# Four neighbouring rows of an expert matrix on each partition: first layer's experts and second layer's down matrix

## The chip, the cores and the metric

The kernel runs on one NeuronCore of a Trainium2 chip. The metric is the device time of one execution in microseconds (us), the median of several. Two numbers of the clock of the matrix engine are used below: it is granted 2.4 GHz or half of that, 1.2 GHz, and the profile writes this as 1.00 and 0.50.

The engines are TensorE (PE: matrix products; PEld is its loading of the stationary operand), VectorE (DVE), ScalarE (ACT), GpSimd (POOL) and SyncE (SP), which issues most DMA transfers. SBUF is the memory on the chip, with 128 partitions; PSUM, in 8 banks, takes the products.

## The reference

A chain of two transformer blocks on 256 tokens of 1024 values, all in float32. Only the two mixtures of experts matter here:

```python
# first layer: 16 experts, each token goes to 2 of them
for e in range(N_EXPERTS):
    h = jax.nn.silu(t @ w_gate[e]) * (t @ w_up[e])
    y = y + gate_dense[:, e:e + 1].astype(t.dtype) * (h @ w_down[e])
...
# second layer: 32 experts, each token goes to 4 of them; one block of tokens of one expert
gu = xb @ w_gu[e] + b_gu[e]
gate, up = gu[:, :D_FF_EXPERT_2], gu[:, D_FF_EXPERT_2:]
gate = jnp.minimum(gate, SWIGLU_LIMIT)
up = jnp.clip(up, -SWIGLU_LIMIT, SWIGLU_LIMIT)
glu = gate * jax.nn.sigmoid(SWIGLU_ALPHA * gate)
return ((up + 1.0) * glu) @ w_down[e] + b_down[e]
```

Each expert has three matrices of 1024 x 1024 floats, 4 MB each. Ahead of each mixture stands a token mixer (attention, retention), a normalization and a router that picks the experts.

## The kernel before

**Phases.** The program is written out by hand, engine by engine, with semaphores between the engines; nothing is reordered by a scheduler. Four phases follow each other: a (the first layer's token mixer, and conditioning for the second), m1 (the first layer's experts), b (the second layer's token mixer), m2 (the second layer's experts).

**The ring.** All weights pass through `ring`, six slots of 2 MB (16 KB on each partition), loaded by SP in the order of their use. SP waits for a slot to be free (L979: `sp.wait_ge(S(f"{m}_free{j}"), i + 1)`), issues the transfer of one tile, and goes to the next. In m1 and m2 a slot holds half a matrix, 512 rows of 1024 floats: slots 0 and 1 gate, 2 and 3 up, 4 and 5 down. In the code these halves are cut by `moe_units` (L299 to L306). Its `(k p)` puts row 128k + p of a half on partition p at place k, so each partition receives four separate rows of 4 KB.

**The expert loop.** `moe` (L659) runs once for each block of up to 64 tokens of one expert; a table of blocks, computed on the chip, gives their number and experts. In this run there are 16 blocks in m1 and 32 in m2. The first block's six tiles are loaded ahead of the loop, those of the others within it. On TensorE one pass does this:

- gate products, first half (L694, slot 0). The stationary operand is a chunk of the gathered tokens (128 rows of the model dimension x 64 tokens, from `xgT`), the moving one 512 columns of the weights. Two products with 64 columns each go into the two halves of a PSUM bank.
- `scatter` (L702): adds the previous block's result to the tokens; VectorE sums it up (L1703).
- gate, second half, and up (L694, slots 1 to 3). In m2 a bias comes first (L686).
- `gather` for the next block (L678): x transposed and picked in one go. For each of the 8 chunks `k` of the model dimension and each of the 2 tiles `t` of tokens, 128x128 values of the tokens are the stationary operand and a matrix of zeros and ones, `pick` (128 x 64), the moving one. The source `src` is `x_rows` in m1 and `n2_rows` in m2.
- the turning (L737): the hidden values `hid` (64 tokens in two halves on 128 partitions, 512 columns) are transposed in four chunks with `tp`, and VectorE copies them to `hidT` (L1752). The values to be transposed are the stationary operand, `ident` the moving one. L741 turns the scatter matrix.
- down products (L694, slots 4 and 5), stationary `hidT`.

A matrix product sums over partitions, so chunk k of the stationary operand has to carry the same 128 rows, in the same order, as place k of the weight tile. In m1 the gathered tokens `xgT` are used as they come. In m2 they are first scaled and shifted by vectors that lie chunk by chunk (`sc2` and `mod`, L1688 and L1692).

The profile records each float32 product as two loads and two multiplies, so the 16 products of a gather are 32 records; a transpose is one of each.

Of the kernel before, what the change touches and what calls it, by code (L numbers as in the profile page):

```python
# [2 lines left out]

# [11 lines left out]
P = 128  # L29
# [9 lines left out]
CAP = 64  # L39
# [81 lines left out]
def two_block_kernel(nc, a, consts, bias_rows, out):  # L121

    with ExitStack() as ctx:
# [59 lines left out]
        ident, ones, before, suffix, flip = C("ident"), C("ones"), C("before"), C("suffix"), C("flip")  # L183
# [24 lines left out]
        pick = B(3, 128, 1536).rearrange("p (t s) -> p t s", t=TC)  # L208
        pick_g = B(3, 256, 1664).rearrange("p (t f s) -> p t f s", t=TC, f=2)
        y_slot, hid, up_1, gate_1 = (B(4, 512, 512 * i) for i in range(4))  # L210
# [88 lines left out]
        def moe_units(m, e):  # L299

            if m == "m1":
                cut = [(w, 0) for w in (a["w_gate"][0], a["w_up"][0], a["w_down"][0])]
            else:
                cut = [(a["exp_w_gu_2"][0], 0), (a["exp_w_gu_2"][0], FF), (a["exp_w_down_2"][0], 0)]
            return [w[bass.ds(e, 1), 512 * i:512 * i + 512, lo:lo + 1024].rearrange("o (k p) f -> p (o k) f", p=P)
                    for w, lo in cut for i in range(2)]  # L306

        MOE = {"m1": (E1, NB1), "m2": (E2, NB2)}
        FIRST_SLOT = {"a": 0, "m1": len(units_a), "b": len(units_a), "m2": len(units_a) + len(units_b)}
# [58 lines left out]
        def _(pe):  # L368
            mm = nc.tensor.matmul
            tp = nc.tensor.transpose  # L370
# [85 lines left out]
            for u, kind in enumerate(("q_sb", "k_sb", "v_sb", "q_dl", "k_dl", "v_dl")):  # L456
                w = part("a", u, KC, 512)
# [201 lines left out]
            def moe(m, src):  # L659
# [5 lines left out]
                XG, G, U, DN, Y0, Y1, PT, HT = banks  # L665
# [6 lines left out]
                weights = [part(m, j, 4, 1024) for j in range(SLOTS)]  # L672
                half = [slice(f * CAP, (f + 1) * CAP) for f in range(2)]

                def gather():
                    for k in range(KC):
                        for t in range(TC):
                            i = mm(XG[:, k * CAP:(k + 1) * CAP], src[:, t, k * P:(k + 1) * P], pick[:, t, :],  # L678
                                   start=(t == 0), stop=(t == TC - 1))
                    i.then_inc(S(f"{m}_gathered"), 1)  # L680

# [33 lines left out]
                with pe.Fori(0, n) as i:  # L715
                    if biased:
                        pe.wait_ge(S(f"{m}_expert"), i + 1)
                        biases()
                    pe.wait_ge(S(f"{m}_xgT"), i + 1)
                    pe.wait_ge(full[0], 16 * i + 16)  # L720
                    product(G, token_chunks, 0, biased)

                    pe.wait_ge(S(f"{m}_y_slot"), i + 1)
                    pe.wait_ge(S(f"{m}_put"), i + 1)
                    scatter(4 * i)
                    pe.wait_ge(full[1], 16 * i + 16)
                    product(G, token_chunks, 1, biased)
                    for j in (2, 3):
                        pe.wait_ge(full[j], 16 * i + 16)
                        product(U, token_chunks, j, biased)  # L730

                    pe.wait_ge(S(f"{m}_pick"), i + 2)
                    gather()

                    pe.wait_ge(S(f"{m}_hid"), i + 2)
                    for c in range(4):
                        ins = tp(HT[:, c * P:(c + 1) * P], hid[:, c * P:(c + 1) * P], ident)  # L737
                    ins.then_inc(S(f"{m}_turned"), 1)
                    pe.wait_ge(S(f"{m}_pick_g"), i + 1)
                    for t in range(TC):  # L740
                        ins = tp(PT[:, t * P:(t + 1) * P], pick_g[:, t, :, :], ident)  # L741
                    ins.then_inc(S(f"{m}_put_ps"), 1)
                    pe.wait_ge(S(f"{m}_hidT"), i + 1)
                    for j in (4, 5):
                        pe.wait_ge(full[j], 16 * i + 16)
                        product(DN, hid_chunks, j)
# [31 lines left out]
            for h in range(RH):  # L778
                n = UB["rv", h]
                by_rows([("rv", h, j) for j in range(4)], "b", n, part("b", n, KC, RV), both, RV)  # L780
                for jp in range(2):
                    ps = open_tile(pe, ("S", h, jp))
                    for j in range(2):
                        for c in range(2):
                            at = (2 * jp + j) * P
                            i = mm(ps[:, j * T:(j + 1) * T], rkT[:, 2 * h + c, at:at + P], rqT[:, 2 * h + c, :],  # L786
                                   start=(c == 0), stop=(c == 1))
# [5 lines left out]
                for t in range(TC):  # L793
                    ps = open_tile(pe, ("ro", h, t))
                    for j in range(4):
                        i = mm(ps[:, :], dec2[:, j, t * P:(t + 1) * P], rv[h % 2][:, j, :], start=(j == 0), stop=(j == 3))  # L796
# [16 lines left out]
            for name, cs in ((("cqT", 0), (0, 1)), (("cqT", 1), (2,))):  # L813
                ps = open_tile(pe, name)
                for c in cs:
                    for t in range(TC):
                        i = tp(ps[:, (c % 2) * T + t * P:(c % 2) * T + (t + 1) * P], cqn[:, t, c * P:(c + 1) * P], ident)
                filled(i, name)
            pe.wait_ge(S("ckn_ready"), 4)
            for c in range(2):  # L820
                ps = open_tile(pe, ("ckT", c))
                for j in range(4):
                    i = tp(ps[:, j * P:(j + 1) * P], ckn[:, j, c * P:(c + 1) * P], ident)
# [3 lines left out]
            for j in range(4):  # L827
                i = tp(ps[:, j * P:(j + 1) * P], kr2[:, j, :], ident)
# [8 lines left out]
            for u in range(2):  # L837
                n = UB["uq", u]
                w = part("b", n, 3, 768)
                landed("b", n)  # L840
                for hp in range(2):
                    name = ("qn", 2 * u + hp)
                    ps = open_tile(pe, name)
                    for j in range(2):
                        f = (2 * hp + j) * (NOPE + ROPE)
                        for k in range(3):
                            i = mm(ps[:, j * T:(j + 1) * T], w[:, k, f:f + NOPE], cqnT[:, k, :], start=(k == 0), stop=(k == 2))
                    filled(i, name)
                for t in range(TC):
                    name = ("qr", u, t)  # L850
                    ps = open_tile(pe, name)
                    for k in range(3):
                        heads = w[:, k, :].rearrange("p (h f) -> p h f", h=4)[:, :, NOPE:]
                        i = mm(ps[:, 0:256].rearrange("p (h f) -> p h f", h=4), cqnT[:, k, t * P:(t + 1) * P], heads,
                               start=(k == 0), stop=(k == 2))
# [4 lines left out]
            w = part("b", n, 2, 2048)  # L860
            landed("b", n)
            for h in range(MH):
                ps = open_tile(pe, ("kn", h))
                for k in range(2):
                    f = h * (NOPE + MV)
                    i = mm(ps[:, :], w[:, k, f:f + NOPE], cknT[:, k, :], start=(k == 0), stop=(k == 1))
# [1123 lines left out]
```

## Time and profile before

| | |
|---|---|
| median of 3 runs | 2461.43 us |
| lowest and highest | 2459.41 and 2461.56 us |
| span of the profiled execution | 2460.9 us |
| TensorE busy, multiplies | 2272.0 us (92%) |
| TensorE busy, loads | 1058.3 us (43%) |
| VectorE, ScalarE, GpSimd busy | 591.0, 291.1, 30.8 us |
| moved by DMA | 713.11 MB, mean 290 GB/s |
| TensorE's mean granted clock | 0.964 |

The costliest group is the expert products of L694: 4608 multiplies, busy for 1021.8 us at a mean of 597 ns, with 37.0 us of idle time ahead of them. The gather of L678 has 1600 of each, 195.8 us for the multiplies and 188.9 us for the loads. Multiplies overlap, so the durations of single ones add up to more than the time that passes; the distance between starts is what counts.

A row of the timeline merges neighbouring instructions of a kind: start, length in us, engine, line, operands with buffer numbers left out (`ring` weights, `pool` the work buffers, `bank` PSUM, `cst` constants), and how many; in brackets the idle time ahead of it and who ended it. A load is written `PEld ... LDWEIGHTS`. Time to landing of a DMA runs from its issue to its last byte, so it includes the queue ahead of it.

### The profile page before, as it was taken

What the parts mean: (1) busy time and instruction counts of PE and PEld (TensorE: products, weight loads), DVE (VectorE), ACT (ScalarE), POOL (GpSimd) and SP (SyncE); (2) the same over time, 40 slices, a digit from 0 to 9 for tenths busy, and PEclk for the clock granted to TensorE, in tenths of its full rate; (3) what the DMA queues carried; (4) which work ended last, traced back from release to release, by engine and by line L of the source; (5) the groups of instructions that cost most, each with busy time, mean ns of one, the idle gap of its engine ahead of it and who ended that gap; (6) DMA issues with size and microseconds to landing.
All of it is one profiled execution on the core that took longest, in us unless ns stands there. A gap on an engine that the chain in (4) does not pass through costs nothing.

```text
span 2460.9 us, 24961 instructions
## 1 busy us (share of the span) xinstructions
PE 2272.0 (92%) x9929; PEld 1058.3 (43%) x9929; DVE 591.0 (24%) x1270; ACT 291.1 (12%) x460; POOL 30.8 (1%) x49
## 2 busy tenths in 40 slices
PE   8997699999998999999999599999999999999997
PEld 6654333333335444445545333333333333333333
DVE  0124311122113300001142422222222222222223
ACT  1411000000011021211032000000000000000000
POOL 1000000000000000000000000000000000000000
PEclk9978699999999999999999689999999999999999
DMA  9483399999997311132412169999999999999993
GB/s 347 174 329 153 131 407 410 410 410 410 410 410 278 137 69 69 54 134 103 172 68 84 68 240 397 399 393 399 399 396 397 400 399 398 396 400 396 398 397 153
DMA packets 198661, 713.11 MB, mean 290 GB/s; under 512 B 6027, under 2 KB 8304, under 8 KB 198208
## 3 DMA queue, kind: packets, MB, share of 16 engines
q1 hardware_dynamic: 196704, 707.20, 73.9%
q0 software_dynamic: 1920, 5.40, 0.7%
q8 instruction: 25, 0.41, 0.1%
q14 instruction: 12, 0.10, 0.0%
HBM read 711.52 MB, written 1.06 MB: 290 GB/s over the span
## 4 chain that ended last, share of the span: by engine, by line
PE 48%; issue 45%; DVE 4%; DMA 2%; ACT 1%; SPq 1%; DVEq 0%; POOL 0%; ACTq 0%; POOLq 0%
PE bank L405 14%; PE bank L694 13%; PE bank L423 6%; PE bank L393 3%; PE bank L678 3%; PE bank L702 2%; PE bank L796 1%; PE bank L479 1%; DMA ring<-in_w_up 1%; SPq L979 1%; ACT pool L1082 1%; PE bank L917 1%; DMA ring<-in_ada_w 1%; PE bank L786 1%; PE bank L873 1%
## 5 line engine op out<-in xcount | busy, mean ns | idle before, releaser
L694 PE MATMUL bank<-ring,pool 128*64 128x512 f32 x4608 | 1021.8, 597 | 37.0 <-DVE pool L1752 34.6
L694 PEld LDWEIGHTS bank<-ring,pool 128*64 128x64 f32 x4608 | 320.2, 137 | 699.7 <-issue 648.8
L405 PE MATMUL bank<-ring,pool 128*128 128x512 f32 (+2 forms) x800 | 335.0, 580 | 5.8 <-DVE pool L1780 4.2
L405 PEld LDWEIGHTS bank<-ring,pool 128*128 128x128 f32 x800 | 152.9, 191 | 182.4 <-issue 168.3
L1703 DVE TENSOR_TENSOR pool<-pool,bank 128x512 f32<-128x512 f32 x200 | 128.5, 684 | 352.3 <-PE bank L702 352.3
L678 PEld LDWEIGHTS bank<-pool 128*128 128x128 f32 x1600 | 188.9, 197 | 47.5 <-issue 43.1
L678 PE MATMUL bank<-pool 128*128 128x64 f32 x1600 | 195.8, 282 | 6.9 <-DVE pool L1679 4.3
L702 PE MATMUL bank<-pool,junk 64*128 64x512 f32 x400 | 142.7, 641 | 40.2 <-DVE pool L1703 38.5
L423 PE MATMUL bank<-ring,pool 128*128 128x512 f32 x320 | 141.0, 602 | 10.2 <-ACTq L1084 5.0
L1196 ACT ACTIVATE pool<-bank 128x512 f32<-128x512 f32 x48 | 28.7, 597 | 845.7 <-PE bank L694 845.7
L1082 ACT ACTIVATE pool<-bank 128x512 f32<-128x512 f32 (+1 forms) x121 | 70.4, 582 | 486.4 <-PE bank L405 175.2
L702 PEld LDWEIGHTS bank<-pool,junk 64*128 64x128 f32 x400 | 44.7, 184 | 137.5 <-DVE pool L1703 95.1
L423 PEld LDWEIGHTS bank<-ring,pool 128*128 128x128 f32 x320 | 61.3, 193 | 87.1 <-issue 75.6
L393 PE MATMUL bank<-pool,ring 128*128 128x256 f32 x384 | 85.3, 385 | 3.0 <-issue 2.1
L393 PEld LDWEIGHTS bank<-pool,ring 128*128 128x128 f32 x384 | 73.9, 193 | 15.1 <-issue 3.1
L1193 ACT ACTIVATE pool<-pool 128x512 f32<-128x512 f32 x32 | 20.2, 630 | 374.8 <-DVE pool L1742 374.8
L686 PE MATMUL bank<-pool,junk 32*64 32x512 f32 x256 | 63.6, 615 | 0.0
L1697 DVE COPY junk<-pool 32x64 f32 (+1 forms) x33 | 6.0, 182 | 230.6 <-PE bank L686 230.6
L1746 DVE TENSOR_SCALAR pool<-bank 128x512 f32<-128x512 f32 x32 | 22.1, 692 | 153.2 <-PE bank L694 153.2
L382 PE MATMUL bank<-cst,pool 128*128 128x128 f32 x176 | 27.3, 319 | 26.9 <-DVEq L1539 9.1
L1739 DVE TENSOR_TENSOR pool<-pool,bank 128x512 f32<-128x512 f32 x16 | 11.0, 687 | 158.4 <-PE bank L694 158.4
L1742 DVE TENSOR_SCALAR pool<-bank 128x512 f32<-128x512 f32 x32 | 22.1, 692 | 93.0 <-PE bank L694 93.0
(318 smaller groups left out, 1185.5 us busy)
## 6 DMA issues: line engine op xcount, KB each, us to landing
ring<-in_exp_w_gu SPq DMA_DIRECT2D x128, 2048.0 KB, 10.8
ring<-in_exp_w_down SPq DMA_DIRECT2D x64, 2048.0 KB, 10.3
ring<-in_w_gate SPq DMA_DIRECT2D x32, 2048.0 KB, 17.2
ring<-in_w_up SPq DMA_DIRECT2D x32, 2048.0 KB, 19.4
ring<-in_w_down SPq DMA_DIRECT2D x32, 2048.0 KB, 16.9
ring<-in_w_in SPq DMA_DIRECT2D x22, 2048.0 KB, 14.5
ring<-in_ada_w SPq DMA_DIRECT2D x12, 2048.0 KB, 11.6
ring<-in_w_out SPq DMA_DIRECT2D x4, 2048.0 KB, 15.5
```

Of the source, the lines that this page charges most:

```text
L382: i = tp(ps[:, c * T + t * P:c * T + t * P + P], src[:, t, (2 * cp + c) * P:(2 * cp + c + 1) * P], ident)
L393: i = mm(ps[:, m * T:(m + 1) * T], w[:, k, (2 * mp_ + m) * P:(2 * mp_ + m + 1) * P], src[:, k, :], start=(k == 0), stop=(k == KC - 1))
L405: i = mm(ps[:, 0:width], src[:, k, t * P:(t + 1) * P], w[:, k, 0:width], start=(k == 0), stop=(k == w.shape[1] - 1))
L423: i = mm(ps[t, f][:, :], srcT[:, kk, t * P:(t + 1) * P], w[:, k, f * 512:(f + 1) * 512], start=(kk == 0), stop=(kk == 4 * units - 1))
L479: i = mm(ps[32 * g:32 * (g + 1), :], silc[:, k, :], part("a", n, KC, 512)[:, k, :], start=(k == 0), stop=(k == KC - 1))
L678: i = mm(XG[:, k * CAP:(k + 1) * CAP], src[:, t, k * P:(k + 1) * P], pick[:, t, :], start=(t == 0), stop=(t == TC - 1))
L686: i = mm(dst[half[f], :], this_expert, bgu_rows[:, at:at + 512], start=True, stop=False)
L694: i = mm(dst[half[f], :], chunks[kk], weights[j][:, k, f * 512:(f + 1) * 512], start=(kk == 0 and not biased), stop=(kk == KC - 1))
L702: mm((Y0, Y1)[f][:, :], put[half[f], t * P:(t + 1) * P], y_slot[half[f], :], start=True, stop=True).then_inc(S(f"{m}_scattered"), 1)
L1082: freed(af(dst, view(ps), func, scale=scale), name)
L1196: act.activation(y_slot, DN[:, :], ACT.Copy).then_inc(S(f"{m}_y_slot"), 1)
L1703: tt(ys, ys, (Y0, Y1)[f][:, :], ALU.add).then_inc(S(f"{m}_added"), 1)
```

## The change

Three edits, in two functions. `moe_units` takes the halves of all m1 matrices, and of the down matrix in m2, as `(p k)`: row 4p + k of a half goes to partition p at place k. A partition thus receives four neighbouring rows, which lie in memory as one run of 16 KB. The gate and up matrix of m2 stays `(k p)`; there a row is also half of a longer one (2048 floats), so four of its halves would not be one run. Place k of such a tile holds rows k, 4 + k, 8 + k and so on. So the gather in m1 takes every fourth column of a half of the tokens, from column k on (`tokens_of`), and the turning in both layers every fourth column of `hid`. The number and order of instructions on each engine is the same.

```diff
@@ moe_units
-            return [w[bass.ds(e, 1), 512 * i:512 * i + 512, lo:lo + 1024].rearrange("o (k p) f -> p (o k) f", p=P)
-                    for w, lo in cut for i in range(2)]
+            lay = {True: "o (p k) f -> p (o k) f", False: "o (k p) f -> p (o k) f"}
+            return [w[bass.ds(e, 1), 512 * i:512 * i + 512, lo:lo + 1024].rearrange(lay[m == "m1" or c == 2], p=P)
+                    for c, (w, lo) in enumerate(cut) for i in range(2)]
@@ moe, on TensorE
+                def tokens_of(t, k):
+
+                    if m == "m2":
+                        return src[:, t, k * P:(k + 1) * P]
+                    return src[:, t, 512 * (k // 4):512 * (k // 4 + 1)].rearrange("p (q c) -> p c q", c=4)[:, k % 4, :]
+
                 def gather():
                     for k in range(KC):
                         for t in range(TC):
-                            i = mm(XG[:, k * CAP:(k + 1) * CAP], src[:, t, k * P:(k + 1) * P], pick[:, t, :],
+                            i = mm(XG[:, k * CAP:(k + 1) * CAP], tokens_of(t, k), pick[:, t, :],
                                    start=(t == 0), stop=(t == TC - 1))
                     i.then_inc(S(f"{m}_gathered"), 1)
...
                     for c in range(4):
-                        ins = tp(HT[:, c * P:(c + 1) * P], hid[:, c * P:(c + 1) * P], ident)
+                        ins = tp(HT[:, c * P:(c + 1) * P], hid.rearrange("p (q c) -> p c q", c=4)[:, c, :], ident)
                     ins.then_inc(S(f"{m}_turned"), 1)
```

## Rows read from the trace of the kernel before

**Rows 1.** The page: span, busy time, the 40 slices, packets of DMA.

```profile
span 2460.9 us, 24961 instructions
...
PE 2272.0 (92%) x9929; PEld 1058.3 (43%) x9929; DVE 591.0 (24%) x1270; ACT 291.1 (12%) x460; POOL 30.8 (1%) x49
...
GB/s 347 174 329 153 131 407 410 410 410 410 410 410 278 137 69 69 54 134 103 172 68 84 68 240 397 399 393 399 399 396 397 400 399 398 396 400 396 398 397 153
DMA packets 198661, 713.11 MB, mean 290 GB/s; under 512 B 6027, under 2 KB 8304, under 8 KB 198208
```

**Rows 2.** Timeline of TensorE, one block of the first layer: start, length, engine, line.

```profile
653.52 3.79 PE L678 MATMUL bank<-pool 128*128 128x64 f32 x32
657.14 0.61 PE L737 MATMUL bank<-cst,pool 128*128 128x128 f32 x4
657.58 0.38 PE L741 MATMUL bank<-cst,pool 128*128 128x128 f32 x2
658.69 10.52 PE L694 MATMUL bank<-ring,pool 128*64 128x512 f32 x48 [0.72 <-DVE pool L1752]
...
672.69 10.52 PE L694 MATMUL bank<-ring,pool 128*64 128x512 f32 x48
683.14 3.79 PE L678 MATMUL bank<-pool 128*128 128x64 f32 x32
```

**Rows 3.** The same timeline, the last two blocks of the first layer.

```profile
710.09 3.65 PE L694 MATMUL bank<-ring,pool 128*64 128x512 f32 x16 [0.69 <-DMA ring<-in_w_up]
713.68 3.79 PE L678 MATMUL bank<-pool 128*128 128x64 f32 x32
...
740.80 3.65 PE L694 MATMUL bank<-ring,pool 128*64 128x512 f32 x16 [0.87 <-DMA ring<-in_w_up]
744.39 3.79 PE L678 MATMUL bank<-pool 128*128 128x64 f32 x32
```

**Rows 4.** Waits in the first layer's loop: total us, times, longest.

```profile
PE bank L694 <- DMA ring<-in_w_up: 1.6, 2, 0.9
```

**Rows 5.** Stretches: length, busy of five engines, granted clock, DMA share, GB/s.

```profile
32.00:42.00 10.00, 10.00 (x47) 8.60 (x47) 0.00 (x0) 0.85 (x2) 0.00 (x0) 1.00 1.05 387
409.00:469.00 60.00, 57.02 (x290) 23.89 (x288) 11.43 (x24) 4.95 (x6) 0.00 (x0) 1.00 1.03 410
2000.00:2100.00 100.00, 95.52 (x476) 38.05 (x474) 25.92 (x52) 9.07 (x11) 0.00 (x0) 1.00 1.01 398
```

**Rows 6.** DMA issues by source: count, KB each, median us from issue to landing.

```profile
ring<-in_w_up SPq DMA_DIRECT2D x32, 2048.0 KB, 19.4
...
cst<-shape_constants SPq DMA_DIRECT2D x1, 1392.5 KB, 21.3
...
ring<-in_mla_w_ukv SPq DMA_DIRECT2D x1, 2048.0 KB, 7.6
...
pool<-in_exp_b_gu POOLq DMA_DIRECT2D x1, 256.0 KB, 3.5
```

**Rows 7.** Timeline of TensorE in the second layer: two gathers, one block apart.

```profile
1924.00 3.79 PE L678 MATMUL bank<-pool 128*128 128x64 f32 x32
...
1955.64 3.79 PE L678 MATMUL bank<-pool 128*128 128x64 f32 x32
```

**Rows 8.** Gather and turning: ns minimum/median/maximum, first and last start, form.

```profile
L678 PEld LDWEIGHTS bank<-pool x1600: 186/192/333, 269.9 to 2433.6; 128*128 128x128 f32 x178
L737 PEld LDWEIGHTS bank<-cst,pool x192: 140/142/199, 301.6 to 2434.0; 128*128 128x128 f32 x192
L737 PE MATMUL bank<-cst,pool x192: 272/273/282, 301.7 to 2434.1; 128*128 128x128 f32 x192
```

**Rows 9.** The first gather of the first layer, and the stretches of two gathers.

```profile
269.90 7.09 PE L678 MATMUL bank<-pool 128*128 128x64 f32 x32 [4.27 <-DVE pool L1679]
...
298.05 3.79 PE L678 MATMUL bank<-pool 128*128 128x64 f32 x32
```

**Rows 10.** Stretch around the first of these gathers, columns as in rows 5.

```profile
262.00:277.00 15.00, 10.01 (x46) 9.61 (x46) 3.51 (x12) 0.00 (x0) 0.00 (x0) 0.50 0.00 1
```

## The prediction

> **What bounds the kernel now.** I read the page first, for the whole: TensorE is busy for 92% of a span of 2460.9 us, and the line of GB/s has two plateaus, about 410 from slice 6 to 12 and about 398 from slice 25 to 39 [rows 1]. These are the two expert loops: 16 blocks of the first layer and 32 of the second, six weight tiles of 2048 KB for each block. Two engines could bound such a loop, TensorE or the DMA, so the next view is the timeline of TensorE alone, and in it the distance between equal instructions of neighbouring blocks. Gather to gather, a block of the first layer takes 683.14 - 653.52 = 29.62 us, with no wait for a DMA in it [rows 2]; one of the second layer takes 1955.64 - 1924.00 = 31.64 us [rows 7]. Six tiles are 12.58 MB. In 29.62 us that is a demand of 424.8 GB/s, in 31.64 us one of 397.7.
>
> The view of stretches shows what the DMA gives: 410 GB/s over 60 us of the first layer's loop, and 398 in the second's [rows 5]. In the second loop that is the demand, so TensorE bounds it and the DMA has spare. In the first loop the queue gives less than is asked: a block needs 12.58 / 410 = 30.69 us on the DMA against 29.62 on TensorE. So the transfers fall behind by 1.07 us for each of the 15 blocks that are loaded inside the loop, 16.0 us in all. A tile's median time to landing of 19.4 us there, against 7.6 us for one tile of the middle part, is that queue [rows 6]. The ring of six tiles swallows nearly all of it: only the last two blocks show TensorE waiting for w_up, with gather to gather 30.54 and 30.71 us in place of 29.62, so 0.92 + 1.09 = **2.0 us** [rows 2, 3]; the view of waits agrees in its order (1.6 us) [rows 4]. The slack of the ring was therefore 16.0 - 2.0 = 14 us.
>
> **The change: the transfers.** All 96 tiles of the first layer and the 64 tiles of exp_w_down_2 go from 512 runs of 4 KB to 128 runs of 16 KB. The other 128 tiles of the second layer keep 4 KB. What does a run cost? Units with runs of 2 KB fill the queue at 387 GB/s, runs of 4 KB at 410 [rows 5]. One of the 16 DMA engines thus needs 2048 x 16 / 387 = 84.7 ns for 2 KB and 4096 x 16 / 410 = 159.8 ns for 4 KB. The second 2 KB cost 75.1 ns, so about 9.6 ns of each run do not depend on its size. My estimate for 16 KB is 84.7 + 7 x 75.1 = 610 ns, or **429 GB/s**. A block of the first layer then takes 12.58 / 429 = 29.3 us on the DMA, under TensorE's 29.62: nothing falls behind, and the 2.0 us go. Nothing else can be gained there, because the next limit is TensorE itself, whose own instructions fill the 29.62 us. In the second layer the gain is nothing: no wait for a DMA lies in its loop, and what hides the transfers is the 31.64 us of TensorE against 30.69 of the DMA. The middle part and the start issue the same transfers as before; the middle's first ones come up to 16 us sooner in the queue, but TensorE begins there with the products of the context, for which no wait for a DMA stands in the trace, so I count nothing. On SP the same number of issues stands in the same order.
>
> **The change: the strided reads.** Row 4q + c of a half matrix now lies on partition q in place c, so the other operand has to follow. Nothing is added: the same instructions in the same order, with another address pattern. In the first layer the gather (L678) loads each 128x128 stationary tile from x_rows with a step of four floats, 16 bytes, where it was contiguous. In both layers the turning of hid (L737) does the same. Vector and scalar work, the products and the scatter are untouched. A gather has 32 load and multiply pairs in 657.14 - 653.52 = 3.62 us, 113 ns a pair, while its moving operand has only 64 columns; a load alone lasts 186 to 192 ns [rows 2, 8]. The pair's pace is thus set by the load, and nothing covers it if it becomes longer: TensorE is the bound, and the gather stands on its path in every block. The loads on the path are 17 x 32 = 544 in the gathers of the first layer (one before the loop, one in each block), and 48 x 4 = 192 in the turnings. The turning takes (657.58 - 657.14) / 4 = 110 ns a pair too, but its load lasts only 140 ns against 273 ns of its multiply [rows 2, 8]. There the load has some 46 ns of spare against that of the gather.
>
> No row of this kernel shows a load with a step, so the price is bounded from both sides. Below: nothing, since the stationary tile has the same 128 columns and is delivered to the array at the same pace; a gain is excluded, as fewer bytes or columns are not read. Above: every load at half its pace. The first gather shows what that looks like, 7.09 us against 3.79, with a granted clock of 0.50 around it, that is 1.2 GHz and not 2.4, after an idle stretch [rows 9, 10]. The difference is 3.30 us for 32 pairs, 103 ns a load. On all 544 loads of the gathers that is +56.0 us; on the 192 of the turnings another +19.8 us if they pay alike, and little if their spare hides it. I take **nothing** as the price. The row that argues for it is the turning: its load of the same 128x128 floats lasts 46 ns less than the gather's [rows 8], so the read side of the load can deliver floats faster than the gather asks for them. The gather's pace has then some room before a slower read shows. I give this little more than even weight against the other end.
>
> Here a rule of the Trainium skill speaks against the change. Its page "SBUF — State Buffer", in "Specifications (TRN2)" and again in "Door 1", says that the memory is read in lines of 16 bytes and that an engine needs at least two hits in a line for full bandwidth; a step of four floats has one. The page names no price; if it halves the load's pace here, the sum ends at +74 us instead of -2. No row of the trace bears on it, and the same note also calls four floats a step that is free.
>
> **The sum.** The profiled execution spans 2460.9 us, the median of the three runs is 2461.4, so what holds for the span holds for the median within 0.5 us. Waits -2.0, loads 0, all else 0: 2461.4 - 2.0 = **2459.4 us**.
>
> **The rivals.**
> *The stepped load is slower.* This ends on the other side. Its place is the gather of the first layer and the turning in both; its price is 544x + 192y, x and y being what a load becomes longer. The wait for w_up of 2.0 us vanishes here too, since a block then takes longer than its transfers. At 103 ns for all loads the time is 2461.4 - 2.0 + 56.0 + 19.8 = 2535; if only the gathers pay, 2515. It decides from 10 to 13 ns a load on, where it outgrows 2.0 + 4.9 us. For it: TensorE is the bound and the load sets the pair's pace. Against it: the faster load of the turning. A part of the full price gives 2468 to 2510.
> *The long runs move slower.* Each engine then reads 16 KB from one place before it goes on, and the trace has few such runs. The slack of 14 us covers 15 blocks up to 29.62 + 14 / 15 = 30.55 us; the time is worse than before by over 0.2% once a block needs more than 31.0 us, a rate under 405 GB/s. At 395 GB/s a block takes 31.9 us and the loop waits 15 x 2.2 - 14 = 19 us: 2479. Against it: from 2 KB to 4 KB the rate rises.
> *The runs stay at 4 KB,* if a run of 16 KB is cut on its way. Then the wait stays and the time is 2461.4. Against it: of the 198661 packets 453 are of 8 KB or more [rows 1], and the loads of the constants (128 rows of 11140 bytes), of ukv (256 runs of 8 KB) and of exp_b_gu (32 of 8 KB) make 416 of them if each run is one packet [rows 6]; the other 37 I take for fetches of instructions. A run of 11 KB was not cut.
>
> **How the numbers follow.** Loads free, or under 10 ns each: 0.48, at 2457 to 2462, whether or not runs stay whole. Full price: 0.30, at 2515 to 2535. A part of it: 0.14. Slower runs: 0.03, around 2479. Something gained that I don't see, over 0.2% or 4.9 us: 0.05. A measurement of this kernel can tell about 0.2% from no change. That makes faster 0.05, same 0.48, slower 0.47. The predicted time is that of the likeliest case, whose own range is 2457 to 2462. Since nearly half lies on the slow side and most of that at its far end, the range for 8 in 10 has to reach there: 2457 to 2536.
>
> **What would show it.** The packets should fall by 96 x 384 + 64 x 384 = 61440, to about 137200; if they don't, the third rival holds. In the first layer's loop the GB/s should rise from 410 towards the demand of 425 if the gather keeps its pace, the wait for w_up should be gone and the time to landing of w_up should fall to about half; if the GB/s stay near 410 with waits, the run's size buys nothing. The step that I trust least is read from two numbers: the pair of the gather (113 ns before) and gather to gather (29.62 us before). If these stand at some 216 ns and 33 us, the first rival has won, and the second layer's 31.64 us tell whether the turning pays as well. A load of the turning at 140 ns would say that it doesn't.

## The result, and the profile after

| | before | changed |
|---|---|---|
| median | 2460.54 us (4 runs) | 2550.23 us (4 runs) |
| lowest and highest | 2459.41 and 2461.56 us | 2549.27 and 2554.47 us |
| span of the profiled execution | 2460.9 us | 2552.7 us |
| TensorE's mean granted clock | 0.964 | 0.940 |

The changed kernel takes 1.0367 times as long, 95% interval 1.0352 to 1.0382: **89.7 us slower**, outside the range of 2457 to 2536 us that was given. (The kernel before has one run more here than ahead of the prediction, which puts its median at 2460.54 in place of 2461.43.) The profiled execution is the slowest of the four.

In the changed kernel the same lines have other numbers: the gather is L671 (L678 before), the products L687 (L694), the scatter L695 (L702), the turning L730 (L737). The page first, as in [rows 1]:

```profile
span 2552.7 us, 24961 instructions
...
PE 2370.3 (93%) x9929; PEld 1134.9 (44%) x9929; DVE 592.5 (23%) x1270; ACT 291.2 (11%) x460; POOL 30.8 (1%) x49
...
PEclk9978789888899899999999959999999999999999
...
GB/s 341 181 330 115 144 383 361 355 344 348 365 373 346 135 132 66 67 78 132 103 165 36 121 36 389 396 396 403 396 398 394 402 395 395 399 397 397 398 397 162
DMA packets 137221, 713.11 MB, mean 279 GB/s; under 512 B 6027, under 2 KB 8304, under 8 KB 116288
```

The packets fall by 61440, as counted, and those of 8 KB or more rise from 453 to 20933, by 160 tiles x 128, so the long runs are real. But the plateau of 410 GB/s is gone, and not upwards: 344 to 373 in slices 8 to 12. TensorE asks for less. PEclk falls to 8 in most of the same slices. The timeline of TensorE over one block and the start of the next shows why, to be held against [rows 2]:

```profile
652.93 7.73 PE L671 MATMUL bank<-pool 128*128 128x64 f32 x32
660.45 1.06 PE L730 MATMUL bank<-cst,pool 128*128 128x128 f32 x4
661.31 0.63 PE L734 MATMUL bank<-cst,pool 128*128 128x128 f32 x2
662.29 11.81 PE L687 MATMUL bank<-ring,pool 128*64 128x512 f32 x48 [0.36 <-DVE pool L1745]
...
677.59 10.52 PE L687 MATMUL bank<-ring,pool 128*64 128x512 f32 x48
688.04 7.73 PE L671 MATMUL bank<-pool 128*128 128x64 f32 x32
```

A gather lasts 660.45 - 652.93 = 7.52 us in place of 3.62, 235 ns a pair in place of 113. The second thing stands in the fourth row: 48 products take 11.81 us in place of 10.52, though nothing in them was changed; the 48 after them (677.59) take 10.52 as before. Over the loop the first 48 take from 11.10 to 12.77 us, the second 48 always 10.52. Gather to gather is now 35.11 us, and over the 15 blocks between the first and the last gather in the loop 35.155 on average. The stretches of a block early in the loop show the clock, columns as in [rows 5]:

```profile
301.00:309.00 8.00, 8.00 (x36) 7.84 (x35) 0.76 (x2) 0.00 (x0) 0.00 (x0) 0.85 1.00 428
310.50:322.40 11.90, 11.87 (x50) 3.71 (x50) 1.15 (x5) 0.60 (x1) 0.00 (x0) 0.88 0.54 198
322.40:336.40 14.00, 13.23 (x59) 4.24 (x57) 2.57 (x4) 1.88 (x2) 0.00 (x0) 1.00 1.01 434
```

The clock is the third number from the end. The first stretch is the gather, 0.85; the second the 48 products after it, 0.88; the third the rest, 1.00. The granted clock thus falls from 2.4 to 1.2 GHz during the gather, and it comes back some microseconds into the products. It is so in the next gathers too: over the first seven of the loop the clock of the gather's 7.5 us is between 0.73 and 0.86.

In the second layer, where only the turning changed, two gathers stand as far apart as in [rows 7], 2047.41 - 2015.77 = 31.64 us:

```profile
2015.77 3.79 PE L671 MATMUL bank<-pool 128*128 128x64 f32 x32
2019.40 0.68 PE L730 MATMUL bank<-cst,pool 128*128 128x128 f32 x4
2019.91 0.38 PE L734 MATMUL bank<-cst,pool 128*128 128x128 f32 x2
2020.94 7.09 PE L687 MATMUL bank<-ring,pool 128*64 128x512 f32 x32 [0.65 <-DVE pool L1745]
...
2047.41 3.79 PE L671 MATMUL bank<-pool 128*128 128x64 f32 x32
```

The turning's pair there takes (2019.91 - 2019.40) / 4 = 128 ns in place of 110. The first down product still starts 5.17 us after the gather (2020.94 - 2015.77), as before. The wait for VectorE in its brackets went from 0.72 to 0.65 us: the 0.07 us came out of that wait. VectorE passes the gathered tokens first (0.69 us) and copies `hidT` right after that (0.68 us), so these two set the start of the product. The turning's load alone became longer too: a median of 219 ns over both layers (shortest 211) where it had 142 (140) [rows 8].

**Where the 91.8 us between the two spans lie.** The first gather starts 2.7 us later (272.58 against 269.90), in a phase that the change does not touch. From the first to the second gather +0.4. In the 15 blocks that follow, 15 x (35.155 - 29.62) = 83.0, of which the gathers are 15 x 3.90 = 58.5 and the rest 24.5, which the section on the granted clock explains. The wait for w_up is gone, -2.0. From the last gather to the next phase +6.5, one gather's 3.90 in it. The next phase +1.4, everything behind it -0.2.

### The profile page after: what moved, and what is told of

It reads as the page before. It is cut to its first block, busy times and chain, and to the rows that moved or that the text cites. A ratio compares the mean times of both kernels' runs of the same rounds, so it can differ in the third digit from the quotient of the medians.

```text
span 2552.7 us, 24961 instructions
## 1 busy us (share of the span) xinstructions
PE 2370.3 (93%) x9929; PEld 1134.9 (44%) x9929; DVE 592.5 (23%) x1270; ACT 291.2 (11%) x460; POOL 30.8 (1%) x49
## 4 chain that ended last, share of the span: by engine, by line
PE 51%; issue 43%; DVE 3%; ACT 1%; DMA 1%; DVEq 0%; POOL 0%; ACTq 0%; POOLq 0%; SPq 0%
PE bank L687 14%; PE bank L392 13%; PE bank L410 5%; PE bank L671 5%; PE bank L380 3%; PE bank L695 2%; PE bank L789 1%; PE bank L466 1%; ACT pool L1075 1%; PE bank L910 1%; DMA ring<-in_ada_w 1%; PE bank L730 1%; PE bank L779 1%; PE bank L866 1%; PE bank L859 1%
## 5 line engine op out<-in xcount | busy, mean ns | idle before, releaser
L687 PE MATMUL bank<-ring,pool 128*64 128x512 f32 x4608 | 1043.2, 607 | 27.3 <-DVE pool L1745 26.4
L687 PEld LDWEIGHTS bank<-ring,pool 128*64 128x64 f32 x4608 | 324.4, 140 | 709.8 <-issue 669.3
L671 PEld LDWEIGHTS bank<-pool 128*128 128x128 f32 x1600 | 251.8, 241 | 47.5 <-issue 43.1
L671 PE MATMUL bank<-pool 128*128 128x64 f32 x1600 | 259.6, 328 | 6.9 <-DVE pool L1672 4.3
L695 PE MATMUL bank<-pool,junk 64*128 64x512 f32 x400 | 142.7, 641 | 40.1 <-DVE pool L1696 38.4
L695 PEld LDWEIGHTS bank<-pool,junk 64*128 64x128 f32 x400 | 44.7, 184 | 137.4 <-DVE pool L1696 95.0
L380 PEld LDWEIGHTS bank<-pool,ring 128*128 128x128 f32 x384 | 75.1, 196 | 15.5 <-issue 3.1
```

The source lines that it names most:

```text
L380: i = mm(ps[:, m * T:(m + 1) * T], w[:, k, (2 * mp_ + m) * P:(2 * mp_ + m + 1) * P], src[:, k, :], start=(k == 0), stop=(k == KC - 1))
L671: i = mm(XG[:, k * CAP:(k + 1) * CAP], tokens_of(t, k), pick[:, t, :], start=(t == 0), stop=(t == TC - 1))
L687: i = mm(dst[half[f], :], chunks[kk], weights[j][:, k, f * 512:(f + 1) * 512], start=(kk == 0 and not biased), stop=(kk == KC - 1))
L695: mm((Y0, Y1)[f][:, :], put[half[f], t * P:(t + 1) * P], y_slot[half[f], :], start=True, stop=True).then_inc(S(f"{m}_scattered"), 1)
```

## The experiments

Two theories were set against each other. **L**: the stepped loads cost the time, the long runs do not. **R**: transfers that write 16 KB into one partition hold up TensorE's reads. A third question was why the clock falls.

### Steps without long runs

Every tile of the first layer comes in four transfers, each with one row of 4 KB per partition. A partition still holds four neighbouring rows, so the loads keep their step. The waits for a tile count to 64 in place of 16. The edit for the first layer, shortened; the second layer keeps the old line:

```diff
-                        sp.dma_start(part(m, j, 4, 1024), src).then_inc(S(f"{m}_full{j}"), 16)
+                        for k in range(4):
+                            sp.dma_start(part(m, j, 4, 1024)[:, k, :], src[:, k, :]).then_inc(S(f"{m}_full{j}"), 16)
```

> The changed kernel, but every tile of the first layer comes as four transfers of one 4 KB row per partition, so the stepped loads stay and the 16 KB runs of the first layer are gone. Theory L (the stepped loads cost the time, the runs do not): about as slow as the changed kernel, 2550 us within 5, a gather pair at 235 ns, gather to gather 35 us. Theory R (long runs landing in the memory hold up TensorE's reads): back to about 2460 us, the pair at 113 ns.

2550.6 us, ratio 1.0364 (1.0347 to 1.0381), the same as the changed kernel with its 1.0367. The gather is 7.52 us, and the mean gather to gather 35.28 against 35.155 us. R falls: without the long runs of the first layer nothing comes back. Two of its gathers, three blocks apart (105.82 / 3 = 35.27 us):

```profile
721.44 7.73 PE L671 MATMUL bank<-pool 128*128 128x64 f32 x32
...
827.26 7.73 PE L671 MATMUL bank<-pool 128*128 128x64 f32 x32
```

### Long runs without stepped gathers

First only the down matrices of both layers lie in long runs, and the gather reads as before:

```diff
-            return [w[bass.ds(e, 1), 512 * i:512 * i + 512, lo:lo + 1024].rearrange(lay[m == "m1" or c == 2], p=P)
+            return [w[bass.ds(e, 1), 512 * i:512 * i + 512, lo:lo + 1024].rearrange(lay[c == 2], p=P)
...
-                    if m == "m2":
-                        return src[:, t, k * P:(k + 1) * P]
-                    return src[:, t, 512 * (k // 4):512 * (k // 4 + 1)].rearrange("p (q c) -> p c q", c=4)[:, k % 4, :]
+                    return src[:, t, k * P:(k + 1) * P]
```

> The long runs for the down matrices of both layers only; gate and up of the first layer lie as before, the gather reads without a step, the turning of hid with one. Theory L: no gather pays, the turning pays 18 ns a pair (128 against 110), and that hides behind VectorE's copies: 2459 to 2461 us. Theory R: a third of the first layer's tiles and of the second's are long, so at least some 20 us slower, 2480.

2461.6 us, ratio 1.0000 (0.9991 to 1.0010), just above the 2459 to 2461 that were expected. The turning's pair takes 128 ns, and gather to gather is 29.62 us in every block, so its step costs the loop nothing, and the median shows no cost clear of the noise. R is out once more.

Then all long runs, with the tokens put in the order of the new rows once. ScalarE writes the copy `x_turned` while the router works, before the loop:

```diff
-                    return src[:, t, 512 * (k // 4):512 * (k // 4 + 1)].rearrange("p (q c) -> p c q", c=4)[:, k % 4, :]
+                    return x_turned[:, t, k * P:(k + 1) * P]
...
+            for t in range(TC):
+                act.activation(x_turned[:, t, :].rearrange("p (h c q) -> p h c q", h=2, c=4),
+                               x_rows[:, t, :].rearrange("p (h q c) -> p h c q", h=2, c=4), ACT.Copy).then_inc(S("root_set"), 1)
```

> The changed kernel with all its long runs, but ScalarE writes once, before the first layer's loop, a copy of the tokens in the order of the new rows, and the gather reads that copy without a step. Theory L: gather pair back at 113 ns, no wait for w_up because the runs of 16 KB keep up with 425 GB/s: 2458.5 us, 2 us under the kernel before. Theory R: still slow, above 2500 us.

2461.73 us, ratio 1.0002 (0.9993 to 1.0012). The gather is back at 3.62 us, and the whole 89.7 us with it: L holds. The loop does what was worked out for the transfers. No wait for w_up is left, every gather to gather is 29.62 us, the queue gives what is asked, and the tile's time to landing falls to 12.2 us from 19.4. The last two gathers, to be held against [rows 3], then the stretch, columns as in [rows 5]:

```profile
711.38 3.79 PE L672 MATMUL bank<-pool 128*128 128x64 f32 x32
...
740.99 3.79 PE L672 MATMUL bank<-pool 128*128 128x64 f32 x32
```

```profile
409.00:469.00 60.00, 57.16 (x290) 24.05 (x288) 11.43 (x24) 5.71 (x7) 0.00 (x0) 1.00 1.01 425
```

The tile in the view of DMA issues, columns as in [rows 6]:

```profile
ring<-in_w_up SPq DMA_DIRECT2D x32, 2048.0 KB, 12.2
```

From the first to the last gather this is 740.99 - 268.54 = 472.45 us against 744.39 - 269.90 = 474.49 before, the 2.0 us that were expected. The median doesn't show them (2458.5 was expected), and a later section says where they went.

### What a step costs

The gather of the kernel before, with its own transfers, with a step of 2, 3 and 8 floats, the rest unchanged; each of the three kernels was run once. With `c` for the step, the columns start at `at`, so that each load still has 128 of them (shortened; only the first layer's gather is changed):

```diff
-                            i = mm(XG[:, k * CAP:(k + 1) * CAP], src[:, t, k * P:(k + 1) * P], pick[:, t, :],
+                    at = c * P * (k // c) % (D - c * P + 1)
+                            i = mm(XG[:, k * CAP:(k + 1) * CAP],
+                                   src[:, t, at:at + c * P].rearrange("p (q c) -> p c q", c=c)[:, k % c, :], pick[:, t, :],
```

> The kernel before with its own transfers; the first layer's gather loads with a step of 2 floats (8 bytes), from windows of 256 columns, so the experts' rows do not fit the tokens: this leaves the right choice of rows out and only the pace is read. Line rule (two hits in a line of 16 bytes are enough): pair 113 ns, gather to gather 29.6 to 30.7 us. Rival, cost in proportion to the lines touched (64 lines for 128 columns, against 32 and 128): pair between 113 and 235 ns, about 150.

> The same with a step of 3 floats (12 bytes; 96 lines for 128 columns; again the wrong rows, only the pace is read). Line rule: most lines have one hit, so near 200 ns. Rival, a threshold at a step of 16 bytes: 113 ns.

> The same with a step of 8 floats (32 bytes; still one line for each column; wrong rows, only the pace is read). Line rule: 235 ns like the step of 4, since the lines are as many. Rival, a cost that grows with the distance: above 300 ns.

From each timeline one gather and the turning behind it (the gather is L685 here, the turning L744). Steps 2, 3 and 8, in this order:

```profile
533.78 3.98 PE L685 MATMUL bank<-pool 128*128 128x64 f32 x32
537.60 0.61 PE L744 MATMUL bank<-cst,pool 128*128 128x128 f32 x4
```
```profile
535.76 6.01 PE L685 MATMUL bank<-pool 128*128 128x64 f32 x32
541.57 1.06 PE L744 MATMUL bank<-cst,pool 128*128 128x128 f32 x4
```
```profile
513.00 7.87 PE L685 MATMUL bank<-pool 128*128 128x64 f32 x32
520.66 1.06 PE L744 MATMUL bank<-cst,pool 128*128 128x128 f32 x4
```

| step in floats | lines of 16 bytes for 128 columns | gather, us | ns a pair | ns a line |
|---|---|---|---|---|
| 1 | 32 | 3.62 | 113 | 3.5 |
| 2 | 64 | 3.82 | 119 | 1.87 |
| 3 | 96 | 5.81 | 182 | 1.89 |
| 4 | 128 | 7.52 | 235 | 1.84 |
| 8 | 128 | 7.66 | 239 | 1.87 |

Two prices explain all five rows: a column costs 0.88 ns, a line of 16 bytes some 1.85 ns, and the load takes as long as the larger sum. At two columns a line the two meet (1.77 against 1.87). That step 8 costs as much as step 4 shows that it is the lines that count and not the distance; step 3, at 182 ns, shows that it is no threshold at 16 bytes. The width of a line comes out of the rows too: with lines of 8 bytes step 2 would cost what step 4 does, and with lines of 32 bytes step 4 would cost about half of step 8.

The step of 8 came out as expected (235, measured 239). For step 3 I had said near 200 ns, and it is 182; for step 2, 113, and it is 119. The rival of step 2 named about 150, which is out; but its form, a cost in proportion to the lines, is what the table shows from 64 lines on, with the columns as a floor. Step 3 needs a word on the clock: the gather shown had 0.92, so some of its pairs went at 1.2 GHz. The same kernel's second gather, at 0.99, took 5.65 us (299.56 to 305.21), 177 ns a pair or 1.84 ns a line.

The price of a line doesn't follow TensorE's clock; that of a column does. The first gather of the changed kernel ran at a granted clock of 0.50, the same level as in [rows 10], and its row has the same length as that of the second, 7.73 us; a single load lasts 329 ns in both. Before, these two were 7.09 and 3.79 us [rows 9]: at 1.2 GHz a pair of 128 columns takes some 216 ns (the 113, and 3.30 us over 32 pairs), just under the 235 of 128 lines. The kernels with other steps agree: their first gathers, at 0.50 too, take 7.09 us at steps 2 and 3, where the columns are the larger sum at 1.2 GHz, and 7.90 at step 8. First the timeline of the changed kernel, then the stretch of its first gather and the loads of its second:

```profile
272.58 7.73 PE L671 MATMUL bank<-pool 128*128 128x64 f32 x32 [4.26 <-DVE pool L1672]
...
301.16 7.73 PE L671 MATMUL bank<-pool 128*128 128x64 f32 x32
308.69 1.06 PE L730 MATMUL bank<-cst,pool 128*128 128x128 f32 x4
```
```profile
272.60:280.30 7.70, 7.70 (x32) 7.51 (x32) 0.00 (x0) 0.00 (x0) 0.00 (x0) 0.50 0.00 0
```
```profile
L671 PEld LDWEIGHTS bank<-pool x32: 309/329/329, 301.2 to 308.4; 128*128 128x128 f32 x32
```

### What the granted clock does

Two kernels ask whether the length of the gather lets the clock fall or the little work in it. The first does each contiguous gather in the loop of the first layer twice (`gather_twice` issues the same 16 products and then calls `gather`; one run):

```diff
-                    gather()
+                    (gather_twice if m == "m1" else gather)()
```

> The kernel before with each gather of the first layer done twice, without a step: as long a gather as the stepped one (7.24 us) but with the array busy twice as often. If the fall of the clock comes with little work in the array and not with the length of the gather: granted clock 1.00 in the loop, the 48 products after it 10.5 us, gather to gather 29.62 + 3.62 = 33.2 us. If length is what counts: clock about 0.86 and 35 us, as in the changed kernel.

The second is the changed kernel with the stepped loads, whose multiplies take the picks twice over, in seven of the eight chunks:

```diff
-                            i = mm(XG[:, k * CAP:(k + 1) * CAP], tokens_of(t, k), pick[:, t, :],
+                            n = 2 if m == "m1" and k < KC - 1 else 1
+                            i = mm(XG[:, k * CAP:(k + n) * CAP].rearrange("p (n s) -> p n s", n=n), tokens_of(t, k),
+                                   pick[:, t, :].unsqueeze(1).to_broadcast([P, n, CAP]),
```

> The changed kernel, but the multiplies of the first layer's gather take their 64 columns twice (128 columns; the second copy falls on a place that is overwritten later, so the values stay). The load of 235 ns hides the longer multiply, only the array is busier. Theory C (the granted clock falls during the stepped gather because the array has little to do, and that costs the products after it): the clock in the loop rises from 0.86 to near 1.00, the first 48 products of a block take 10.5 us again where they take 11.3 to 12.8, the gather stays at 7.5 us; 15 to 25 us faster than the changed kernel, about 2530. Rival D (the products are slow for another reason, such as the DMA or the load's own aftermath): unchanged within 5 us.

The gather done twice, its timeline of TensorE and a stretch of 60 us in the loop:

```profile
529.13 3.79 PE L685 MATMUL bank<-pool 128*128 128x64 f32 x32
532.76 3.74 PE L678 MATMUL bank<-pool 128*128 128x64 f32 x32
536.33 0.61 PE L744 MATMUL bank<-cst,pool 128*128 128x128 f32 x4
536.77 0.38 PE L748 MATMUL bank<-cst,pool 128*128 128x128 f32 x2
537.87 10.52 PE L701 MATMUL bank<-ring,pool 128*64 128x512 f32 x48 [0.72 <-DVE pool L1759]
```
```profile
409.00:469.00 60.00, 57.73 (x318) 27.90 (x315) 8.98 (x17) 4.96 (x6) 0.00 (x0) 1.00 0.97 383
```
The same two views of the wide one (gather L672, products L689, scatter L697, turning L732):

```profile
504.01 10.52 PE L689 MATMUL bank<-ring,pool 128*64 128x512 f32 x48 [0.65 <-DVE pool L1747]
514.46 1.13 PE L697 MATMUL bank<-pool,junk 64*128 64x512 f32 x4
516.37 1.72 PE L697 MATMUL bank<-pool,junk 64*128 64x512 f32 x4 [0.78 <-DVE pool L1698]
518.01 10.52 PE L689 MATMUL bank<-ring,pool 128*64 128x512 f32 x48
528.47 7.68 PE L672 MATMUL bank<-pool 128*128 128x128 f32 x32
535.98 0.68 PE L732 MATMUL bank<-cst,pool 128*128 128x128 f32 x4
```
```profile
409.00:469.00 60.00, 57.81 (x255) 29.04 (x252) 8.98 (x17) 4.96 (x6) 0.00 (x0) 1.00 0.94 396
```

Both have a gather about as long as the changed kernel's, 7.20 and 7.51 us. Both keep the clock at 1.00, and their 48 products take 10.52 us again. Gather to gather they need 33.19 and 33.52 us where the changed kernel needs 35.155; 33.52 is the 29.62 of before and the 3.90 of the longer gather, with nothing left over. So length is not what lowers the clock. Between the wide kernel and the changed one the loads are the same, and only the multiplies beside them are longer: in this loop the clock falls where a long load leaves the array little to multiply. It falls with step 3 too: its loop has a mean clock of 0.93 from 409 to 469 us and its last blocks take 34.13 us, 2.3 more than its longer gather explains; with step 2 the clock stays at 1.00 and a block takes 29.82. The wide kernel's median is 2519.25 us, ratio 1.0230 to before (1.0213 to 1.0247): 31 us under the changed one with more work in it. I had expected 15 to 25 us. The loop's share is 24.5 us. The end of the loop and the next phase had lost some 4 us by the clock too, as the ledger above shows, and from the first gather to the second the wide kernel needs 26.13 us (267.72 to 293.85) against 28.58: its first products come at the full clock earlier. Together that is 31 us.

### How fast the runs move

In both of these the first layer's loop leaves out half of its expert products (k 1 and 2 of each half matrix), so that the transfers bind. One is the kernel before, the other the one with long runs and the copied tokens; each was run once.

> The kernel before with half of the first layer's expert products left out, so that its loop is bound by the transfers of 4 KB runs: 410 GB/s, 30.7 us gather to gather.

> The same half of the products left out, with the long runs of 16 KB and the copy of the tokens made once, so that its loop is bound by the transfers of 16 KB runs. The fit of the prediction: 429 GB/s, 29.3 us gather to gather. Rival, no gain beyond 4 KB: 410 GB/s, 30.7 us.

Stretches in the loop, columns as in [rows 5], of the kernel before without half of its products, then of the other:

```profile
400.00:500.00 100.00, 67.54 (x334) 29.63 (x333) 19.87 (x44) 7.43 (x9) 0.00 (x0) 0.95 1.03 410
```
```profile
400.00:500.00 100.00, 79.47 (x332) 37.01 (x331) 19.80 (x43) 8.03 (x10) 0.00 (x0) 0.82 1.01 428
500.00:600.00 100.00, 71.02 (x308) 30.89 (x306) 19.82 (x40) 9.31 (x11) 0.00 (x0) 0.91 1.01 429
```

410 GB/s with runs of 4 KB and 428 to 429 with 16 KB, both with the DMA engines busy and TensorE with idle time; its clock falls at times, to means of 0.95, 0.82 and 0.91. Gather to gather the first settles at 30.72 us, the mean of its alternating 30.71 and 30.73; the second varies from 28.0 to 31.0 us, with 29.37 on average over its last 13 blocks, where 29.3 was expected. The fit of the prediction, 9.6 ns for each run and 75.1 ns for each 2 KB, gave 429.

### Where the two microseconds went

> The kernel with the long runs and the tokens copied once, a second time. In its first profile the loop was 2.0 us shorter, as worked out, but the 18 us from the last gather to the next phase and the phase itself were 2.3 us longer, with a granted clock of 0.72 there against 1.00 before. If that fall of the clock belongs to this kernel, it shows again (about 659.2 us from the end of the loop to the second layer's first gather) and the median stays level with before. If it is chance, it is there in some executions of either kernel, and more rounds bring the ratio towards 0.9992.

> The kernel before, unchanged, profiled a second time as the control of the run above. If the fall of the clock after the first layer's loop is chance, it may show here too; if it belongs to the kernel without the wait for w_up, this shows 657.8 us for that stretch again. Median 2461.3 us, ratio 1.000.

The kernel with long runs and copied tokens: 2463.7 us, ratio 1.0000 (0.9992 to 1.0009); the kernel before once more: 2462.03 us, ratio 1.0001 (0.9993 to 1.0010). The 2.0 us lie at the edge of what can be told apart here. The profiles tell more. The stretch of 12 us at the end of the loop, first of the kernel before in its two profiles, then of the other in two (from two starts, since the loops end some us apart: they lie 9.6, 12.8, 11.0 and 10.5 us behind the last gather; in the second profile of the kernel before the clock is 1.00 from 9.8 us on as well. The clock is the third number from the end):

```profile
754.00:766.00 12.00, 9.64 (x41) 5.20 (x38) 6.41 (x10) 0.60 (x1) 0.00 (x0) 1.00 1.05 387
```
```profile
752.00:764.00 12.00, 10.21 (x42) 7.41 (x43) 8.68 (x15) 0.15 (x1) 0.70 (x1) 1.00 1.05 386
```
```profile
752.00:764.00 12.00, 9.65 (x27) 5.02 (x24) 6.91 (x11) 0.60 (x1) 0.00 (x0) 0.72 1.05 387
```
```profile
754.00:766.00 12.00, 9.65 (x29) 4.78 (x24) 6.46 (x10) 0.60 (x1) 0.00 (x0) 0.72 1.05 387
```

In both profiles of the kernel with long runs, and in that of the down matrices only, the clock falls here, and from the last gather to the next phase 18.5 us pass in place of 17.6 (in the timelines 759.51 - 740.99 against 761.95 - 744.39); the phase behind it takes 659.1 to 659.3 us in place of 657.8 and 657.9. That is 2.2 to 2.4 us given back for 2.0 won. The work in this stretch is the same, with the same idle times of some 0.7 to 0.9 us between its pieces. The changed kernel shows the long phase too (659.25); the wide one, which also has the long runs, doesn't (657.6), nor does the one with steps and 4 KB runs (657.8). So it isn't the run as such. The kernel with a step of 2 settles that: its runs are the 4 KB of before, and its clock is 0.72 from 754 to 766 us all the same, with 18.71 us from the last gather to the next phase and 659.34 in it. What it shares with the others is that its loop has no wait for w_up at its end (gather to gather 29.82 us to the last). Of the kernels whose blocks take 29.6 to 29.8 us, the three without that wait lose the clock here, the one with long runs and copied tokens in both of its profiles, and the kernel before, with the wait, keeps it in both of its own. Why the clock falls for one arrival at this point and not for another stays open.

## Why the prediction was wrong

**The transfers: right.** The bound of each loop, the queue that fell behind by 1.07 us a block, the slack of 14 us and the wait of 2.0 us all held up in the loop. The rate of 429 GB/s was met at 428 to 429, the packets came down to 137221. The kernel with only the down matrices in long runs is one more test of the slack: its loop moves 416 GB/s, so a block needs 30.25 us and falls behind by 0.63, 9.4 us over the loop, under 14; it shows no wait, with 29.62 us from gather to gather. The third rival, runs that stay at 4 KB, and the second, long runs that move slower, are both out.

**The loads: wrong, and this is the step that failed.** I took nothing as the price, with a chance of 0.48, on the strength of one row: the turning's load was 46 ns shorter than the gather's, "so the read side of the load can deliver floats faster than the gather asks for them". Contiguous floats it can, since four come with each line. The row said nothing of a new line for each float. The measured price is 122 ns a load in the gather (235 against 113), and the steps 2, 3, 4 and 8 show its law.

**The upper end: too low.** The 103 ns of "every load at half its pace" came from a gather at half the clock. That was the nearest row, but another mechanism: there the price was that of the columns at 1.2 GHz, here it is that of the lines, and 128 of them take 235 ns at either level. Sixteen gathers in the loop at +3.90 us are 62.4 us, where the bound had 52.8.

**The turning: right place, wrong price.** I gave it 0 to 19.8 us. The sign named for a turning that doesn't pay, a load still at 140 ns, didn't come: the load takes 219. Its pair became longer too, 128 ns against 110 in the second layer, but 0.07 us a block vanished in the wait for VectorE. The spare that I looked for between load and multiply was not the cover; VectorE's two copies were.

**The clock: missing.** I wrote that 2.0 us and the loads were all. But a slower load leaves the array with less to do in the same time, and the granted clock fell in every block of the loop. That is 24.5 us of the 91.8 in the loop and some 4 behind it, which no term of the sum held. With 62.4 for the gathers and the turnings at zero, the first rival would have come to about 2522 us; it is the clock that carries the result beyond 2536, the end of the range. Nor would free loads have brought 2459.4: the kernel with the tokens copied once has them, wins its 2.0 us in the loop, gives 2.2 to 2.4 back by the clock behind it, and stands at 2461.73 and 2463.7 us, level with before.

The rule of the Trainium skill that was weighed, in "SBUF — State Buffer", "Specifications (TRN2)" and "Door 1" (lines of 16 bytes, at least two hits for full bandwidth), agrees with the trace in the point that matters: two hits cost 119 against 113 ns, one costs 235, somewhat more than the half pace that I tried for it. Its remark in "Door 1" that four floats are a step that is free does not: that is the step of this kernel.

## What to carry over

A layout that makes the transfers longer moves a step into some other operand. Look first at the load of TensorE that has to take it: where a load sets the pace of small products, count the 16-byte lines that it touches beside its columns, and take the dearer sum. If the strided read is needed, pay for it once, outside the loop and on an engine that is idle, as the copy of the tokens did.

A bound by TensorE is a bound at its present clock. Where a change makes TensorE wait or starve inside its own instructions, add the products behind it at 1.2 GHz to the sum.

And the gain has to be there in the first place: the whole wait that longer runs could remove was 2.0 us of 2461, and that stood in the timeline ahead of any estimate.

## What the runs showed of the hardware

- A load of float32 stationary values in products costs 0.88 ns a column at 2.4 GHz or some 1.85 ns for each line of 16 bytes, whichever sum is larger, at steps of 1, 2, 3, 4 and 8 floats. The first price nearly doubles at 1.2 GHz (113 to some 216 ns a pair); the second is the same at both levels (a row of 7.73 us and loads of 329 ns at 0.50, a row of 7.68 us and loads of 329 ns at 1.00 in the wide kernel). In the transposes of the second layer, with the same step of four floats, the pair takes 128 ns, 1.0 ns a line. Why a line costs less there was not tried.
- ScalarE seems to pay a like price. Its two copies of 128x1024 floats with a step of four took 3.91 us, 2006 ns each, 1.9 to 2.0 ns for each float; a contiguous pass of the same 128x1024 floats from the same memory, a square with a sum (L1203), took 1048 ns in the same kernel, 1.0 ns for each. These are two kinds of pass, and the step was not varied. The two copies in the timeline of ScalarE, kernel with long runs and copied tokens:

```profile
248.39 3.91 ACT L1196 ACTIVATE pool<-pool 128x1024 f32<-128x1024 f32 x2
```

- More work in the array made the kernel faster: with the same loads, doubling the columns of the gather's multiplies took 31 us off; the granted clock in the loop was 1.00 where it had been 0.86 (409 to 469 us).
- The DMA queue moved 387, 410 and 429 GB/s with runs of 2, 4 and 16 KB.
- The first gather of the first layer, ahead of which TensorE does the same in all kernels, starts between 264.96 and 272.58 us in the profiles of this study. In the two that open this document the clock was granted differently in the same phase: 0.50 for the changed kernel and 0.79 for the one before at 104 to 108 us, 0.78 and 0.50 at 120 to 124 us. A spread of 7.6 us is larger than the 2 us in dispute, and it may be where single runs come to differ; it was not tested.
